# Even stage of a transformer kernel on one core: projection halves spread over the attention steps, weight splits moved, output banks swapped, ScalarE's copies ahead of its exponentials

## What is computed

```python
def even_mixer(h, w_in, ...):
    z = h @ w_in                       # 1024 x 2760
    q_a, c_kv, q_i, k_i, w_i, q_b, k_b, v_b = jnp.split(z, ...)
    o_a = dsa_attention(...)           # 8 heads: softmax over the 64 keys that an index score selects
    o_b = diff_attention(...)          # 4 heads: softmax(q0 k0) - lam * softmax(q1 k1), then v, then rms norm
    return jnp.concatenate([o_a, o_b], axis=-1) @ w_out
```

## Time and profile before

| | |
|---|---|
| median of 3 runs | 1419.68 us (1418.42 to 1419.91) |
| profiled execution, its own time | 1419.04 us |
| its span | 1417.2 us |
| mean granted clock of TensorE | 0.995 |
| PE, DVE, ACT, POOL busy | 98%, 72%, 52%, 6% |
| even attention, from its first scores to the first product of `out2` | 824.45 to 865.39, 40.94 us |
| odd attention, likewise | 1135.51 to 1172.94, 37.43 us |
| chunks of `out2`'s weights, issue to landing, median | 5.1 us |

### The profile page before, as it was taken

The page is one execution under the profiler, slowest core; times in us unless marked ns, Lnnn a source line. Parts: engine busy times, 40 slices in busy tenths (PEclk is TensorE's granted clock), DMA queues, the critical chain, the costliest instruction groups (busy, mean ns, idle before and its releaser), DMA issues.

```text
span 1417.2 us, 20234 instructions
## 1 busy us (share of the span) xinstructions
PE 1390.5 (98%) x7888; PEld 1186.0 (84%) x7888; DVE 1014.3 (72%) x1533; ACT 740.5 (52%) x1136; POOL 81.6 (6%) x90
## 2 busy tenths in 40 slices
PE   8999999999999999999999999999999999999997
PEld 6899888888888997888888767888888878888886
DVE  5565778777765657977787675887676866886665
ACT  5564455555445554555555564654445664654443
POOL 0000001000000000211111001000000000000000
PEclk9999999999999999999999989999999999999999
DMA  8844355555565334666655431458866523365652
GB/s 300 238 141 144 125 179 192 194 179 186 171 209 177 120 119 161 207 202 210 210 184 180 146 119 61 134 179 220 222 197 208 164 90 104 109 204 185 201 192 75
DMA packets 154438, 242.31 MB, mean 171 GB/s; under 512 B 4524, under 2 KB 107068, under 8 KB 154079
## 3 DMA queue, kind: packets, MB, share of 16 engines
q1 hardware_dynamic: 150626, 227.23, 49.5%
q0 software_dynamic: 3712, 13.77, 3.7%
q10 hardware_dynamic: 4, 0.01, 0.0%
HBM read 239.03 MB, written 1.97 MB: 170 GB/s over the span
## 4 chain that ended last, share of the span: by engine, by line
PE 90%; DVE 4%; DMA 2%; ACT 2%; issue 1%; POOL 0%; SPq 0%; DVEq 0%; ACTq 0%; POOLq 0%
PE ps L948 19%; PE ps L914 16%; PE ps L921 16%; PE ps L918 16%; PE ps L951 10%; PE ps L1026 3%; PE ps L1114 3%; DMA raw<-in_w_in 2%; PE ps L1080 2%; PE ps L1095 1%; DVE wlo L2122 1%; PE ps L988 1%; PE ps L990 1%; PE ps L989 1%; ACT whi L1652 1%
## 5 line engine op out<-in xcount | busy, mean ns | idle before, releaser
L2122 DVE TENSOR_TENSOR wlo<-raw,whi 128x1024 fp32r<-128x1024 f32 (+1 forms) x432 | 538.4, 1257 | 194.9 <-ACT whi L1652 194.2
L1652 ACT CAST whi<-raw 128x1024 fp32r<-128x1024 f32 (+1 forms) x432 | 446.6, 1042 | 272.9 <-PE ps L921 172.3
L948 PE MATMUL ps<-act,whi 128*128 128x512 f32 x1184 | 324.9, 395 | 1.2 <-DVE wlo L2122 0.9
L914 PE MATMUL ps<-whi,mhi 128*128 128x512 f32 (+2 forms) x688 | 236.4, 392 | 1.9 <-DVE mlo L2149 1.9
L948 PEld LDWEIGHTS ps<-act,whi 128*128 128x128 f32 x1184 | 204.8, 189 | 31.9 <-DVE wlo L2122 1.6
L921 PE MATMUL ps<-whi,mlo 128*128 128x512 f32 (+2 forms) x688 | 231.4, 385 | 0.0
L918 PE MATMUL ps<-wlo,mhi 128*128 128x512 f32 (+2 forms) x688 | 231.2, 385 | 0.0
L951 PEld LDWEIGHTS ps<-act,wlo 128*128 128x128 f32 x1184 | 182.6, 189 | 25.7
L951 PE MATMUL ps<-act,wlo 128*128 128x256 f32 x1184 | 189.4, 281 | 0.0
L914 PE MATMUL ps<-whi,act 128*128 128x256 f32 (+1 forms) x512 | 169.1, 330 | 0.8 <-DVE wlo L2122 0.8
L921 PE MATMUL ps<-whi,act 128*128 128x256 f32 (+1 forms) x512 | 165.3, 323 | 0.0
(11 more groups left out here) (272 smaller groups left out, 1470.0 us busy)
## 6 DMA issues: line engine op xcount, KB each, us to landing
raw<-in_mlp_w SPq DMA_DIRECT2D x64, 1024.0 KB, 5.3
raw<-in_w_up SPq DMA_DIRECT2D x44, 1024.0 KB, 5.2
raw<-in_w_in SPq DMA_DIRECT2D x39, 1024.0 KB, 5.2
raw<-in_w_down SPq DMA_DIRECT2D x22, 1024.0 KB, 4.9
raw<-in_ev_w_in SPq DMA_DIRECT2D x10, 1024.0 KB, 5.2
raw<-in_w_out SPq DMA_DIRECT2D x8, 1024.0 KB, 5.1
raw<-in_xa_wkv SPq DMA_DIRECT2D x4, 1024.0 KB, 5.4
raw<-in_ev_w_out SPq DMA_DIRECT2D x4, 1024.0 KB, 5.1
```

What stands on the lines that cost most here:

```text
L914: nc.tensor.matmul(o, hi[:, kx, rows_], wh[:, k, c0:c0 + w], start=first and h == 0 and k == 0 and (tt == 0 or at[1] == 0), stop=False)
L948: nc.tensor.matmul(both, wh[:, k, w], act2[:, kx].rearrange("p i n -> p (i n)"), start=kx == 0, stop=False)
L1652: nc.scalar.copy(whi[:, m % HL, 0:w], raw[:, n % RAW, h * w:h * w + w]).then_inc(hi_done, 1)
L2122: nc.vector.tensor_tensor(wlo[:, m % HL, 0:w], raw[:, n % RAW, h * w:h * w + w], whi[:, m % HL, 0:w].bitcast(F32), ALU.subtract).then_inc( ...
```

## The change

In the even stage: `in2_half(last, h)` is issued at units 0, 2, 4, 6, one per step, where all four stood at units 0 to 3. Behind units 10, 12, 14 and 16 one spare product into bank 3 is added. The wait for the last group of keys moves from unit 1 to 7, the wait for the projection's output from 5 to 9, ACT's own taking of it from 5 to 8. Of the splits for `out2`, split 0 stays with split 1 gone from its place; 1 and 2 move to units 26 and 30 (DVE: 27 and 31), and 3 comes only behind the heads, ahead of the split of half 4. Differential heads go to banks 6 and 2, sparse heads to 7 and 3, two turned groups of `out2` to 6 and 2. In ACT's `attention` for pairs, the copy stands ahead of the two exponentials; this function is shared with the odd stage.

```diff
-EVEN_SPLITS = {2: 1, 4: 2, 6: 3}
-EVEN_LOWS = {3: 1, 5: 2, 7: 3}
+EVEN_FILL = (0, 2, 4, 6)
+EVEN_SPARES = range(10, 17, 2)
+EVEN_SPLITS = {2: 0, 26: 1, 30: 2}
+EVEN_LOWS = {3: 0, 27: 1, 31: 2}
...
+        def out_beside(col):
+            return lambda qt: ((7, 3)[qt], col)
...
-                           ..., i, lambda qt, i=i: ((7, 3)[qt], P * (i // 2)), False))
+                           ..., i, out_at(P * (i // 2)), False))
...
-                           ..., 2 * HB + i, out_at(HD * i), True))
+                           ..., 2 * HB + i, out_beside(HD * i), True))
...
             if key[0] == "o2" and key[1] % 2 == 0 and key[2] >= 2:
-                return (7, 3)[key[2] - 2]
+                return (6, 2)[key[2] - 2]
...
                     def even_waits(i):
-                        if i < 4:
-                            in2_half(last, i)
+                        if i in EVEN_FILL:
+                            in2_half(last, EVEN_FILL.index(i))
+                        if i in EVEN_SPARES:
+                            spare(1, 3)
                         if i == 0:
                             groups_at(99)
-                        if i == 1:
+                        if i == 7:
                             taken("qkb", 3)
-                        if i == 5:
+                        if i == 9:
                             pe.wait_ge(ev_act, evs_act2(l, "in2", order[-1]))
...
                     if each:
                         each(i)
                         each(i + 1)
+                    j = i - 2 * PAIR_LAG
+                    if j >= 0 and copied_by[u0 + j][0] == "act":
+                        act.wait_ge(at_x, u0 + j + 2)
+                        act.wait_ge(at_o, u0 + j - 4)
+                        nc.scalar.copy(values_of(u0 + j, us[j], True), turned_pair(u0 + j, us[j])).then_inc(at_ya, 1)
                     if i < n:
                         exponents(i)
                         exponents(i + 1)
-                    j = i - 2 * PAIR_LAG
-                    if j >= 0 and copied_by[u0 + j][0] == "act":
-                        act.wait_ge(at_x, u0 + j + 2)
-                        act.wait_ge(at_o, u0 + j - 4)
-                        nc.scalar.copy(values_of(u0 + j, us[j], True), turned_pair(u0 + j, us[j])).then_inc(at_ya, 1)
...
-                    if i == 5:
+                    if i == (8 if even else 5):
                         in2_out(order[-1])
...
-                        ..., ps[:, (7, 3)[qt], :].rearrange("p (h d) -> p h d", d=P),
+                        ..., ps[:, (6, 2)[qt], :].rearrange("p (h d) -> p h d", d=P),
```

More of the change, by code:

```diff
@@ L509, in even_heads @@
                            lambda nk, i=i, b=b: qT[b:b + 64, 4 + i // 2, 0:nk], causal, band_of(HA + i // 2),
-                           lambda s, i=i: proj[:, s, 2248 + P * (i // 2):2248 + P * (i // 2) + P], i, lambda qt, i=i: ((7, 3)[qt], P * (i // 2)), False))
+                           lambda s, i=i: proj[:, s, 2248 + P * (i // 2):2248 + P * (i // 2) + P], i, out_at(P * (i // 2)), False))
             return hs
@@ L518, in dsa_heads @@
                            lambda nk, i=i, b=b: qT[b:b + 64, 12 + i // 2, 0:nk], causal, band_of(i),
-                           lambda s, i=i: proj[:, s, HD * i:HD * i + HD], 2 * HB + i, out_at(HD * i), True))
+                           lambda s, i=i: proj[:, s, HD * i:HD * i + HD], 2 * HB + i, out_beside(HD * i), True))
             return hs
@@ L1722, in attention @@
                         each(i + 1)
-                    if i < n:
-                        exponents(i)
-                        exponents(i + 1)
                     j = i - 2 * PAIR_LAG
@@ L1731, in attention @@
                         nc.scalar.copy(values_of(u0 + j, us[j], True), turned_pair(u0 + j, us[j])).then_inc(at_ya, 1)
+                    if i < n:
+                        exponents(i)
+                        exponents(i + 1)
             def spread_row(key, l):
@@ L2729, in diff_out @@
                         link(nc.vector.reciprocal(r, total))
-                        nc.vector.tensor_tensor(heads_of(o_nat, qt, 512, HB, P), ps[:, (7, 3)[qt], :].rearrange("p (h d) -> p h d", d=P),
+                        nc.vector.tensor_tensor(heads_of(o_nat, qt, 512, HB, P), ps[:, (6, 2)[qt], :].rearrange("p (h d) -> p h d", d=P),
                                                 r.unsqueeze(2).to_broadcast([P, HB, P]), ALU.mult).then_inc(diff_taken, 1)
```

## The result

The median of four runs is 1410.21 us (1410.03 to 1410.52). The kernel before, run beside it, has 1419.05 us (1417.06 to 1419.91), so the ratio is 0.994, with a 95% interval of 0.9923 to 0.9957: 8.84 us faster. The median of three known before the prediction was 1419.68; from there it is 9.47.

The account below looks back on a forecast made before the run. In the even stage, PE's idle 2.1 us and 10.2 us at half clock, plus both stages' value products waiting for ScalarE's copy, bound the kernel. 3.6 + 1.8 + 1.6 = 7.0 off 1419.68 gives 1412.7; range 1411.3 to 1416.8.

Parts of the forecast that it names:

- Both losses: Even stage, from 832 us on: PE idle for 2.1 us, then 10.2 us at half clock holding 5.1 us of work.
- part 1: Even stage, joint steps: one half per step and the splits moved give 3.6 us; bounds 1.4 and 4.3.
- the terms at nothing: Even stage: moved splits, their later transfers and the changed banks each cost 0; without cover the splits would cost 3.6.
- part 4: Copies ahead of ScalarE's exponentials: 1.8 us gained in the even stage, 1.6 us in the odd stage.
- the smaller rest: Even stage, copies: a short wait at unit 20 and the step from unit 16 at full clock, put at 0.3.
- The two long waits: Even stage: two of PE's waits for ScalarE's copy, the later before 861.67, giving 0.5 and 1.0 us.
- I take the middle, 1.6 us: Odd stage, copies: gain put between PE's waits of 1.2 and its weight loads' waits of 1.9.
- the bounds of 8.4: Both stages: upper end of the total gain from all terms, 3.9 to 8.4 us.
- (a): Even stage: the clock falls once all the same, costing 5.1 us, 1417.8; chance 0.07.
- (b): Even stage: clock falls at the new gap near 827 and stays low until step 16; 4.0 slower, 1423.7; chance 0.04.
- (c): Copies give nothing because another wait, VectorE's, stands right behind theirs; 1416.1; chance 0.09.
- (d): Even stage: the moved splits come onto the path and all 3.6 is given back; 1416.3; chance 0.06.

Follow-up runs that it names:

- clock_only: The kernel before with only seven spare products added in PE's gaps (three behind unit 5, four behind unit 6): 1417.67 us, ratio 0.9986.
- no_swap: The changed kernel with ScalarE's copies put back behind the exponentials: 1414.47 us, ratio 0.9964 to the kernel before.
- splits_only: The kernel before with only the splits moved as in the change; halves and copies stay in their old places: 1414.4 us, ratio 0.9966.
- no_spares: The changed kernel without the four spare products: 1410.95 us, ratio 0.9932 to the kernel before.
- swap_only: The kernel before with only ScalarE's copies moved ahead of its exponentials: 1413.95 us, ratio 0.996.
- before_third: The kernel before, unchanged, run again for a third trace: 1419.77 us.

## Why the prediction was right or wrong

**Right: what bounds the stage.** Both losses were there, though the second was not worth its 5.1 us: holding the clock alone gave 2.0 (`clock_only`). The clock is full in every slice, the fifth step starts at 834.40 and the ninth at 840.43, and the output product at 858.66. Counted from the start of the stage the fifth step was forecast at 10.75 and came at 10.38, the ninth at 16.85 and 16.41. The one gap is at 827.70, 1.23 us long, as the forecast of 828.1 had it. Without the copies the ninth is at 16.76, so part 1 gave 20.45 - 16.76 = 3.7 up to there (forecast 3.6), and 0.2 behind.

**Right: the terms at nothing.** The moved splits cost nothing: from step 20 to the output product, all of it at full clock, `no_swap` takes 16.74 us, `splits_only` 16.74, and the kernel before, which has no splits there, 16.73. The transfers went out at 852.6 and 865.0 (forecast 854 and 867), and the output product waits for none. That the banks cost nothing was not tried alone; with the spread halves and the moved waits, and without spares, they make 0.1 (34.21 against 34.11).

**Wrong: the size of part 4.** The step that failed is "the smaller rest (a short wait at unit 20, and the step from unit 16 at full clock) I put at 0.3", and with it "bounds 1.3 (PE's own idle without the first) and 2.2"; it measured 0.98, and the even stage's part 2.45. The two long waits were right: 0.59 and 0.90 against 0.5 and 1.0. The rest was 0.36 + 0.25 + 0.37 = 0.98, in steps 12, 16 and 20; the first of them lies where part 1 was added up without any wait for the copy. I read the products' row, 1.6 in 3, and left aside the weight loads' row, 3.1 in 6, which holds two of the three small waits. The third, 841.21 in `no_swap`, has no row in the kernel before: its step stands in the half-clock stretch. In the odd stage I had both rows, 1.2 and 1.9, and the step "I take the middle, 1.6 us" failed; it was 1.90. Part 4 gave 4.35 instead of 3.4.

**Wrong: the range had no term for the runs.** The two stages gave 8.2 against 7.0, which lies inside the bounds of 8.4 and would have made 1411.5. The rest of the 9.47 came from outside, and that it pushed the time out of the range rather than into it is chance: 0.64, by which the profiled execution was below the median from which I subtracted, 0.43 in the start of the stage, 0.31, by which the new median is below the new profile, less 0.1 elsewhere. I named the first of these and gave it no room in the range. The new traces of the kernel before show what differs from run to run: the half clock lasts 10.2 us in two and 13.6 in one of three, and the stage begins up to 1.5 us apart, latest where the clock was also at half near 27 us. A change that removes a stretch whose length varies gains more against the median than against one of its shorter profiles.

**The rivals.** (a) The clock did not fall. The Trainium skill, "TensorE: Matmul & The Clock Gate", section "A second HAM failure mode: psum-queue depth-cycling", tells of a kernel (bf16, 512 columns) whose small idles between groups of products made it swing. The trace does not show this here: PE has 3.70 of 4.00 us busy from 836 on, and in steps 6, 10 and 14 its weight loads wait 0.3 to 0.5 us for VectorE's joined product, at a clock of 1.00. `no_spares` keeps 1.00 too, with 3.33 of 4.00 from 837 on. Ahead of each fall in the even stage stands a stretch like that of the earlier trace rows: 1.89 of 4.00 us in the kernel before and in `swap_only`, 1.85 in the second trace of the kernel before, 2.60 of the last 4.00 before the fall at 836.1 in the third. It is not all that can stand there: the falls near 27 us have a PE that was busy throughout ahead of them. The price of 5.1 in (a) was too high: from step 8 to step 20 the kernel before takes 12.73 us, 10.2 of them at half clock, and the changed kernel 9.38 at full clock. By my estimate from these, a fall of that length would have cost about 3.3 us. (b) The gap at 827.7, which was to start it, did nothing. (c) is excluded by `no_swap`, (d) by the steps behind unit 20. What I had not seen is that part 1 is nearly all the splits: spreading the halves over units 0, 2, 4 and 6, which I took for half of the cure, gives nothing once VectorE's two splits in a row are gone (34.21 against 34.11). Over units 0, 1, 2 and 4 it gives 0.42 (33.69 against 34.11).

## What to carry to other kernels

Read the waits of the weight loads beside those of the products: here the loads' waits for the copy, less those with another engine late right behind, were about what the steps got back (1.90 us of waits in the odd stage, 1.90 gained; 2.54 in the even stage, 2.45 gained), and the products' rows were shorter or missing. A stretch at half clock hides waits that stand behind it, and its length varies from run to run, so a change that removes it needs a second profile of the kernel before, and a range that holds the difference. Where the clock falls behind an idle stretch of PE, look first for what the engine it waits for could do later; spare products mended the clock alone (2.0 us, where moving the splits gave 4.15).

## What the runs showed of the hardware

- The same kernel, with the same steps ahead of it (step 8 at 11.47 or 11.48 each time), has the half clock for 10.2, 10.2 and 13.6 us in three profiles, and `swap_only` has it for 6.8. During it PE was busy for nearly all of the time (9.98 of 10.20 us in the kernel before).
- In four of 14 traces the granted clock is also at 0.50 for 3.4 us between 26 and 31 us, behind 7.00 us of a PE that was busy throughout (`before_third`); the other ten have 1.00 there with the same work.
- Holding the clock at full gave back 2.0 us (`clock_only`) where the products at half clock had cost 5.1, since PE then waited for VectorE and ScalarE.
- A spare product of 512 columns costs the stage 0.18 or 0.21 us in steps 12 and 16, about the 0.22 that I had worked out from the earlier trace rows, and 0.05 or nothing in steps 10 and 14: 0.43 for four.
